# One modulation load ahead of the v weights, and one wait for each u weight, at the edge between the first MLP and the gate

## The reference

```python
def ada_modulation(c, w, b):
    m = jax.nn.silu(c) @ w + b
    return jnp.split(m, 6, axis=-1)

def sq_relu_ffn(h, w1, w2):
    return jnp.square(jax.nn.relu(h @ w1)) @ w2

def chunk_mlp_mixer(h, idx, p):
    z = jax.nn.gelu(h @ p['w_in'])
    u, v = jnp.split(z, 2, axis=-1)
    v = rmsnorm(v, p['g_v'])
    g = sgu_mix(u.reshape(shp), v.reshape(shp), p['w_s'], p['b_s'], idx).reshape(B, T, SGU_WIDTH)
    return g @ p['w_o'], v

x = x + gate2 * sq_relu_ffn(modulated_norm(x, norm2_g, shift2, scale2), w1, w2)   # end of layer 0
h = modulated_norm(x, norm1_g, shift1, scale1)                                     # start of layer 1
```

## Time and profile before

| What | Value |
|---|---|
| Median of 3 runs | 2989.66 us |
| The profiled execution | 2997.97 us |
| Its span | 2996.1 us |
| Mean granted clock of TensorE | 0.965 of full |
| PE busy | 2787.4 us (93%) |
| DVE busy | 1852.8 us (62%) |
| ACT busy | 1147.4 us (38%) |
| POOL busy | 885.6 us (30%) |
| Packets on q1 | 22.8% of the 16 DMA engines' span |
| Packets on q0 | 4.7% |

### The profile page before, as it was taken

The page is one execution under the profiler, slowest core; times in us unless marked ns, Lnnn a source line. Parts: engine busy times, 40 slices in busy tenths (PEclk is TensorE's granted clock), DMA queues, the critical chain, the costliest instruction groups (busy, mean ns, idle before and its releaser), DMA issues.

```text
span 2996.1 us, 47585 instructions
## 1 busy us (share of the span) xinstructions
PE 2787.4 (93%) x15902; PEld 2470.9 (82%) x15902; DVE 1852.8 (62%) x3070; ACT 1147.4 (38%) x2375; POOL 885.6 (30%) x970
## 2 busy tenths in 40 slices
PE   7788888779996999999999998899999999999998
PEld 4777776679885889898888887788889989999897
DVE  4566676645553666766666676422567676776775
ACT  3355455424443233333334332222334344343331
POOL 1122011036662002424343435100002343443435
PEclk8889999979997999999999999999999999999999
DMA  5212111222213432222222238513531111111117
GB/s 215 78 67 88 47 52 69 77 70 66 66 59 125 150 113 75 80 77 77 77 77 77 77 95 203 145 43 99 173 122 43 42 52 46 42 42 42 53 60 141
DMA packets 126068, 254.87 MB, mean 85 GB/s; under 512 B 16548, under 2 KB 66628, under 8 KB 122632
## 3 DMA queue, kind: packets, MB, share of 16 engines
q1 hardware_dynamic: 117016, 221.70, 22.8%
q0 software_dynamic: 8944, 31.86, 4.7%
HBM read 213.39 MB, written 40.12 MB: 85 GB/s over the span
## 4 chain that ended last, share of the span: by engine, by line
PE 64%; DMA 2%; DVE 1%; SPq 1%; issue 0%; ACT 0%; POOL 0%; POOLq 0%; DVEq 0%; ACTq 0%
PE psum L102 21%; PE psum L103 20%; PE psum L104 20%; PE psum L149 1%; DMA half_mod_w<-in_ada_w_ffn 1%; PE psum L2880 1%; PE psum L3034 0%; DMA half_w_raw<-in_w_o 0%; DMA scratch_x_mid<-half_out 0%; PE psum L3045 0%; PE psum L3008 0%; DVE half_out L2615 0%; DVE half_w_lo L2484 0%; DVE gate_wv L2766 0%; DMA gate_wu_raw<-in_cm_w_in 0%
## 5 line engine op out<-in xcount | busy, mean ns | idle before, releaser
L102 PE MATMUL psum<-half_hT_hi,half_w_hi 128*128 128x384 f32 x1536 | 518.0, 337 | 0.0
L104 PE MATMUL psum<-half_hT_hi,half_w_lo 128*128 128x384 f32 x1536 | 514.4, 335 | 0.0
L103 PE MATMUL psum<-half_hT_lo,half_w_hi 128*128 128x384 f32 x1536 | 514.1, 335 | 0.0
L2367 POOL TENSOR_TENSOR half_acc<-half_acc,half_upd 128x512 f32<-128x512 f32 x312 | 420.7, 1365 | 54.3 <-ACT half_upd L2134 48.5
L102 PE MATMUL psum<-half_w_hi,half_s_hi 128*128 128x512 f32 x1040 | 409.7, 394 | 0.0
L103 PE MATMUL psum<-half_w_lo,half_s_hi 128*128 128x512 f32 x1040 | 406.5, 391 | 0.0
L104 PE MATMUL psum<-half_w_hi,half_s_lo 128*128 128x512 f32 x1040 | 405.5, 390 | 0.0
L2582 DVE TENSOR_TENSOR half_acc<-half_acc,psum 128x512 f32<-128x512 f32 x416 | 280.9, 683 | 93.5 <-PE psum L104 93.5
L2117 ACT ACTIVATE half_s_raw<-psum 128x384 f32<-128x384 f32 (+2 forms) x256 | 97.6, 407 | 591.0 <-PE psum L104 591.0
L102 PEld LDWEIGHTS psum<-half_hT_hi,half_w_hi 128*128 128x128 f32 x1536 | 289.0, 188 | 5.6 <-issue 0.3
L103 PEld LDWEIGHTS psum<-half_hT_lo,half_w_hi 128*128 128x128 f32 x1536 | 289.1, 188 | 1.2
(11 more groups left out here) (395 smaller groups left out, 5844.2 us busy)
## 6 DMA issues: line engine op xcount, KB each, us to landing
half_w_raw<-in_w SPq DMA_DIRECT2D x64, 512.0 KB, 4.1
half_w_raw<-in_w SPq DMA_DIRECT2D x128, 256.0 KB, 3.5
half_mod_w<-in_ada_w_ffn SPq DMA_DIRECT2D x64, 384.0 KB, 3.1
patt_mod_w<-in_ada_w_att SPq DMA_DIRECT2D x16, 1024.0 KB, 4.9
half_m<-scratch_mixT SPq DMA_DIRECT2D x18, 512.0 KB, 5.2
satt_lT_raw<-in_cacheT SPq DMA_DIRECT2D x32, 256.0 KB, 3.0
satt_l_raw<-in_cache POOLq DMA_DIRECT2D x32, 256.0 KB, 2.9
half_w_raw<-in_w_o SPq DMA_DIRECT2D x16, 512.0 KB, 5.5
```

What stands on the lines that cost most here:

```text
L102: pe.matmul(out, a_hi, b_hi, start=first, stop=False)
L103: pe.matmul(out, a_hi, b_lo, start=False, stop=False)
L104: return pe.matmul(out, a_lo, b_hi, start=False, stop=last)
L2367: pool.tensor_tensor(part, part, a.upd[n % UPDS][:], ALU.add).then_inc(a.added, 1)
```

## The change

Four edits are made:

- On SP, the load of modulation quarter 1 of the last slab moves ahead of the wait for the first `half_acc` stores and of v blocks 0 and 1.
- On ACT, the one wait for all nine `half_out` stores ahead of `split_w(8)` goes. `split_w(n)` for n from 8 waits for the store of tile n - 8 instead. Tiles 2 to 5 now count on `acc_stored[0]` and share one bound, so blocks 10 to 13 wait for all four of them. Tiles 6, 7 and 8 share another.
- On SP, the wait for all nine stores moves behind `load_w(12)`. Where it stood, SP now waits until DVE has finished the last output product (`out_ready`).
- On POOL, `store_out` signals the semaphore that `out_stored` names.

```diff
+def out_stored(a, t):
+
+    if t < 2:
+        return a.stored[t], 16
+    return (a.acc_stored[0], 16 * (4 + 4)) if t < 6 else (a.stored[2], 16 * (TT - 6))
+
 def wait_stored(eng, a):
 
-    for n, tiles in enumerate((1, 1, TT - 2)):
-        eng.wait_ge(a.stored[n], 16 * tiles)
+    for t in (0, 1, 2, 6):
+        eng.wait_ge(*out_stored(a, t))
@@
+            later_mod_w(a, LAST, 1)
             sp.wait_ge(a.acc_stored[0], 16 * 4)
             load_w(0)
             load_w(1)
-            later_mod_w(a, LAST, 1)
             load_w(2)
             later_mod_w(a, LAST, 2)
@@
             store_mod(a, LAST)
-            wait_stored(sp, a)
+            sp.wait_ge(a.out_ready, V * PLAIN + 1)
             load_table(sp, g.scale_t, io["mod"], 1, SCALE1, 0, g.tab_in)
@@
             load_w(12)
+            wait_stored(sp, a)
             load_w(13)
@@
             def split_w(n):
                 act.wait_ge(g.raw_in[n % 4], 16 * (n // 4 + 1))
+                if n >= KT:
+                    act.wait_ge(*out_stored(first, n - KT))
@@
             gate_hT(1)
-            wait_stored(act, first)
             for n in range(8, 12):
                 split_w(n)
@@
-                pool.dma_start(layer_io[a.layer][1][t], a.out[t][:], accum_op=ALU.add).then_inc(a.stored[min(t, 2)], 16)
+                pool.dma_start(layer_io[a.layer][1][t], a.out[t][:], accum_op=ALU.add).then_inc(out_stored(a, t)[0], 16)
```

## The result

The changed kernel takes 2973.05 us in the median of six runs (2968.69 to 2980.67), against 2989.78 us for the kernel before in six runs of the same comparison. The ratio is 0.9947, with a 95% interval of 0.9936 to 0.9959. The forecast was 2971.9 us, from 2968 to 2980.5. In a later comparison it took 2973.93 us against 2990.74, a ratio of 0.9937 (0.9923 to 0.9950).

The account below looks back on a forecast made before the run. PE, busy for 93% of the span, was taken as the bound. Gains of 7.3 us (quarter 1's wait) and 10.5 us (u-weight waits) sum to 17.8, so 2989.66 - 17.8 = 2971.9 us, range 2968 to 2980.5.

Parts of the forecast that it names:

- Quarter 1 ahead: Last slab: quarter 1 takes v block 0's place in the queue, lands at 1835.4, leaving PE 2.1 us of wait.
- What is late next: Last slab: v blocks 0 and 1 land one place later; output v = 0 starts near 1845.5, gain 7.3 us.
- ACT's waits: ACT's splits of u blocks 8 to 11: sooner splits gain nothing themselves but serve SP's last loads; cost nothing.
- SP's wait: SP's loads after the last output: tables start 10.2 us sooner, all three `gate_wu_lo` waits go, gain 10.7 less 0.2.
- The last slab after v = 0: Blocks 3 and 4 overlap the next loads by about 1.5 us; costed at nothing, failure showing as a `gate_wv` wait.
- second edge: PE's three waits for low parts of u weights before `gate_T(2)`, priced at 10.7 us with the lower clock.
- The sum: Whole kernel: both gains act in series, 7.3 + 10.5 = 17.8 us.
- first edge: PE's wait for modulation quarter 1 in the last slab, priced at 10.4 us with the lower clock; forecast gain 7.3.
- Rival A: DMA engines, not SP's waits, set when blocks 12 to 15 land; 7.3 plus perhaps 2 us, 2980.5; chance 0.12.
- B: Quarter 1 or block 0 stays late: gain 2 to 4 us there, 10.5 at the u weights, 2976; chance 0.11.
- C: Everything comes back: quarter 1 in time, block 0 no later; 10.4 + 10.7 = 21.1 us, 2968.6; chance 0.04.
- D: Small loads on q1 alternate with q0's stores, block 12 lands 9.5 us later, kernel some 3 us slower; chance 0.03.

Follow-up runs that it names:

- e5: Changed kernel with quarter 1's load between v blocks 0 and 1 instead of ahead of both; 2978.72 us in one run.
- e6: Changed kernel with the last three of nine `half_acc` stores cut to 128 of 1,024 columns, so the result is incomplete; 2969.22 us in one run.
- e4: Kernel before with only ACT's waits made finer, one for each u block's own stores; 2989.57 us, ratio 1.0002.
- e3: Kernel before with only SP's wait for the nine stores moved behind u block 12; 2981.31 us, ratio 0.9973.
- e9: Changed kernel with DVE's splits of v blocks 6 and 7 later and u blocks 12 to 15 ahead of small loads; 2970.30 us, ratio 0.9934.
- e7: Changed kernel with DVE's splits of v blocks 6 and 7 behind outputs 15 and 16; 2972.31 us, ratio 0.9937.
- e8: Changed kernel with DVE's splits of v blocks 5, 6 and 7 behind outputs 15, 16 and 17; 2970.48 us, ratio 0.9937.
- e11: Changed kernel with the load of v block 4 moved behind that of x tile 0; 2973.08 us, ratio 0.9945.
- e2: Changed kernel without the move of quarter 1's load, which stays where the kernel before had it; 2978.50 us, ratio 0.9962.
- e1: Kernel before with only quarter 1's load moved ahead of the store wait and v blocks 0 and 1; 2980.86 us, ratio 0.9970.

## Why the prediction was right, step by step

**Quarter 1 ahead.** Forecast: landing at 1835.4, a wait of 2.1 us. On the scale of the kernel before (add 5.5) it landed at 1819.38 + 9.8 + 5.5 = 1834.7, and the wait was 1.37. In the other runs with this order it was between 0 and 1.5, in some of them with 0.3 to 1.3 us for quarter 2 behind it. All eight profiles lie under the forecast of 2.1, so the share of the place was sized too long: 10.6 us from issue to landing, measured 7.8 to 10.0. That the place sets the landing is shown by e5; that the stores beside the queue matter at this edge is shown by e6.

**What is late next.** Block 0 was to land at 1839.2 and hold `relu(3)` and u = 5 for 0.5 us. It landed at 1819.79 + 13.2 + 5.5 = 1838.5, and the wait for `half_s_raw` is 0.35 us. T1's gain was 8.4 us for a forecast of 7.3. Of the 1.1 us between them 0.7 is the shorter wait for quarter 1, and the rest is mostly the 0.5 us allowed for a dip of the clock, which did not come.

**ACT's waits.** Costed at nothing by themselves and as a service to SP. e4 and e3 agree.

**SP's wait.** The tables went 10.2 us sooner and block 12 went 12.5 us after the first of them, for a forecast of 12.3. Block 15's parts were ready at 1897.8, when PE needed them at 1894.17 + 21 x 0.227 = 1898.9, a slack of 1.1 us where 0.7 was forecast. All three waits went, as forecast.

**The last slab after v = 0.** This step failed. The overlap of blocks 3 and 4 with the next loads was costed at nothing, with a wait for `gate_wv` as its sign. It showed elsewhere, at x tile 0. Before, blocks 3 and 4 did not wait for the stores. They stood behind the load of quarter 2, which waits until PE has used quarter 1. They went 10.0 us ahead of PE's quarter 2 (1852.79) and were in 4.4 us ahead of it. Now SP waits 6.2 us for the stores first. They go 2.5 us ahead of quarter 2 (1838.88), and block 4 is in 3.1 us after it. Before and after, with the tile's landing, which follows 0.1 us after quarter 2:

```profile
1842.77 0.91 SPq L1944 DMA_DIRECT2D gate_wv_raw<-in_cm_w_in  x2
...
gate_x<-scratch_x_mid SPq DMA_DIRECT2D x1, 512.0 KB, 3.2
...
1836.35 0.80 SPq L1951 DMA_DIRECT2D gate_wv_raw<-in_cm_w_in  x2
...
gate_x<-scratch_x_mid SPq DMA_DIRECT2D x1, 512.0 KB, 5.6
```

POOL's first sum needs the tile and DVE's second output. The output is done 4.2 us after quarter 2 in every run. So the sum starts 4.4 us after quarter 2 before and 5.7 now, and the whole delay is the tile's:

```profile
1857.15 2.71 POOL L2447 TENSOR_TENSOR gate_x<-gate_x,half_out 128x1024 f32<-128x1024 f32 x1 [26.48 <-DVE half_out L2615]
...
1844.61 2.39 POOL L2456 TENSOR_TENSOR gate_x<-gate_x,half_out 128x1024 f32<-128x1024 f32 x1 [19.43 <-DMA gate_x<-scratch_x_mid]
```

DVE works without a pause from there on, and two of its instructions beside POOL's sums are slower than before, 1.55 against 0.50 us and 3.54 against 3.19. Before, then after:

```profile
1859.64 0.50 DVE L2567 TENSOR_TENSOR half_s_lo<-half_s_raw,half_s_hi 128x256 fp32r<-128x256 f32 x1
...
1861.00 3.19 DVE L2766 TENSOR_TENSOR gate_wv<-gate_wv_raw,gate_wv 128x1024 fp32r<-128x1024 f32 x1
...
1845.73 1.55 DVE L2576 TENSOR_TENSOR half_s_lo<-half_s_raw,half_s_hi 128x256 fp32r<-128x256 f32 x1
...
1847.80 3.54 DVE L2775 TENSOR_TENSOR gate_wv<-gate_wv_raw,gate_wv 128x1024 fp32r<-128x1024 f32 x1
```

The rows show a pattern that makes this exact. The subtraction for `half_s_lo` starts 6.8 to 6.9 us after quarter 2 in every run. Where POOL's first sum is running then, DVE ends 0.3 us after the sum does, whenever that is: at 7.35 us for a sum that ends at 7.07 (before), at 8.40 for 8.12 (after), at 9.18 for 8.90 (e9). Where DVE starts first, by 0.06 us in e7 and 0.07 in e8, it takes 0.42 us. The next subtraction, on a v weight, does the same with POOL's second sum: it ends 1.1 us after it (before, after and e9), and took 1.21 us in e11, where it began first. Of e7 and e9:

```profile
1847.70 0.42 DVE L2576 TENSOR_TENSOR half_s_lo<-half_s_raw,half_s_hi 128x256 fp32r<-128x256 f32 x1
1847.76 2.61 POOL L2456 TENSOR_TENSOR gate_x<-gate_x,half_out 128x1024 f32<-128x1024 f32 x1 [19.82 <-DMA gate_x<-scratch_x_mid]
...
1841.78 2.39 POOL L2456 TENSOR_TENSOR gate_x<-gate_x,half_out 128x1024 f32<-128x1024 f32 x1 [19.88 <-DMA gate_x<-scratch_x_mid]
1842.12 2.33 DVE L2576 TENSOR_TENSOR half_s_lo<-half_s_raw,half_s_hi 128x256 fp32r<-128x256 f32 x1
```

So the tile's 1.4 us make POOL's sum end 1.05 us later, DVE makes `gate_hT_lo` 1.06 us later, and PE waits 1.04 us longer; T2 is 0.7 us longer than in e2. e1 has the same longer wait without the second edge. e2, e5 and e6 have 2.3 us, and in each of them the tile lands in 3.2 or 3.3 us and POOL starts at 4.4. e7's shorter wait and e9's longer one, and e11's 1.86, follow from which of the two engines began first at each sum. What slows the tile itself is not taken apart: blocks 3 and 4 are in flight beside it, quarter 3 and x tile 1 follow at once, and e11 shows that moving block 4 alone does not help.

**The sum.** 17.8 us was forecast. The stretches gave 8.4 + 10.0 = 18.4 in the first profile and 9.1 + 8.8 = 17.9 in the second, the medians 16.7 and 16.8. The two misses nearly cancel, 1.1 us more at the first edge and 0.5 less at the second, and that the sum comes so close is partly luck. The profiled execution was forecast at 2980.2 and took 2973.6; 5.5 of these 6.6 us arose ahead of the first edge. *Rival A* (one edge only) is refuted by e2's T2 of 65.45, *B* by e1's T1, *C* by the waits that are left. *D*, the small loads beside the stores, did not decide. In its working 9.5 us lost against 7.3 gained make 2.2 us, not some 3. A small part of it may be there: block 12 landed 5.7 us after its issue and not 3.5, and the issue of the eight blocks varied from 5.8 to 9.5 us where the stores still ran. The longest of these uses up the slack in e11.

## What to carry to other kernels

When a load is late, look at what stands ahead of it on its queue and what runs beside it on the others. Here one place in the queue was worth 2.6 us, and the last stores of another queue most of what was left of the edge. A wait that holds many instructions behind it is priced by the last of them that someone needs: moving SP's wait behind the small loads gave 9.1 of the second edge's 10.7 us, while finer waits on ACT, which looked like the larger edit, gave little without it. When a stall is taken out, whatever did not move with it (here two loads tied to earlier stores) now falls on work that did. And when the profile names a releaser that had long been done, look up when the other things waited for came: in e11 that was the tile, 1.3 us after the output it named.

## What was not expected of the hardware

SP took between 5.6 and 9.5 us for the same eight issues of 8 KB: 5.55, 5.89 and 5.94 in e1, e4 and before, where they wait for the stores to end, and 5.79 to 9.49 in the kernels where the stores still run (5.79 in e2, 6.20 and 7.25 in the two profiles of the changed kernel, 9.49 in e11). Why it varies so much was not found. One and the same subtraction on DVE took 0.42 us when it began 0.06 us ahead of a POOL sum (e7), and 2.33 when it began 0.34 us behind one (e9). At the `gate_hT_lo` wait the lower clock followed waits of 2.3 us and more in all ten profiles that had one, and none of the four of 1.9 us and less. How long it lasted varied from about 3 us to about 10 (e1). And the profiled span varied by some 5 us in stages that no kernel changed, with the granted clock of the first 1400 us at 0.94 in one execution and 0.95 in another.
